# Where the last stage runs, in which order a sampled tile comes, and which router operand stands still

## What is computed

```python
# token mixer B: u, vb are two 512-wide projections of x
vn  = layer_norm(vb, ln_v_g, ln_v_b)
mix = einsum('gts,bcsgd->bctgd', tril(w_spatial), vn in chunks of 128) + b_spatial   # prompt
mix = w_spatial[:, 0, 0] * vn + b_spatial[:, 0]                                      # sampled
gm  = u * mix
merged = sigmoid(ga + gate_bias[0]) * (attn_out @ w_branch_a) + sigmoid(gb + gate_bias[1]) * (gm @ w_branch_b)
h = layer_norm(ALPHA * x + merged @ w_o, ln1_g, ln1_b)
# channel mixer: top-1 of 4 groups, top-2 of its 8 experts
lg = h @ w_router_group + b_router_group
le = h @ w_router_expert + b_router_expert
f  = sum over the two chosen experts of weight * (silu(h @ w_gate) * (h @ w_up)) @ w_down
y  = layer_norm(ALPHA * h + f, ln2_g, ln2_b)
```

## Time and profile before

| what | us |
|---|---|
| median of 3 runs (lowest, highest) | 1595.13 (1594.96, 1598.93) |
| the profiled execution | 1585.32 |
| its span, first to last instruction | 1583.8 |
| TensorE busy | 1440.6 |
| VectorE busy | 733.8 |
| TensorE's mean granted clock | 0.951 |

### The profile page before, as it was taken

One profiled execution on the slowest core, in us unless ns is written; L12 is line 12 of the kernel. 1 busy time (PEld: TensorE's weight loads), 2 busy tenths in 40 slices (PEclk: granted clock), 3 DMA queues, 4 the chain that ended last, 5 costly groups with the idle time before them and its releaser, 6 DMA issues. The chain is left out here.

```text
span 1583.8 us, 17679 instructions
## 1 busy us (share of the span) xinstructions
PE 1440.6 (91%) x5634; PEld 778.2 (49%) x5634; DVE 733.8 (46%) x1662; ACT 283.7 (18%) x620; POOL 254.5 (16%) x308
## 2 busy tenths in 40 slices
PE   7999999799979999998998898999299999999944
PEld 2444444344346666665776564555244444444410
DVE  0101023788888889932659445555311111111127
ACT  0100122112121111111564200000011111111112
POOL 3131000033310000101351000111111111111103
PEclk9999999799989999999999999999599999999967
DMA  9221001400021112201331394000189898989639
GB/s 313 63 64 33 15 15 67 126 0 1 0 96 69 60 60 86 76 28 38 98 109 57 114 355 195 27 27 27 45 339 351 339 349 337 354 334 348 249 92 249
DMA packets 74504, 221.88 MB, mean 140 GB/s; under 512 B 16738, under 2 KB 42338, under 8 KB 65098
## 3 DMA queue, kind: packets, MB, share of 16 engines
q1 hardware_dynamic: 58170, 184.64, 33.3%
q0 software_dynamic: 14992, 35.90, 6.4%
q10 hardware_dynamic: 1280, 0.53, 0.2%
HBM read 190.56 MB, written 38.84 MB: 145 GB/s over the span
## 5 line engine op out<-in xcount | busy, mean ns | idle before, releaser
L1713 PE MATMUL main_ps_experts<-w_gate_up,main_e_rowsT 128*128 128x512 f32 x512 | 227.7, 598 | 1.2 <-DVE main_e_rowsT L1812 1.2
L234 PE MATMUL ps_front<-front,x_all 128*128 128x512 f32 (+1 forms) x448 | 183.8, 566 | 1.7 <-ACT wi L364 1.7
L854 DVE TENSOR_SCALAR_CACHE_REDUCE front<-score,bound 128x384 bf16<-128x384 f32 (+2 forms) x198 | 174.2, 942 | 19.2 <-DVE bound L880 18.9
L1713 PEld LDWEIGHTS main_ps_experts<-w_gate_up,main_e_rowsT 128*128 128x128 f32 x512 | 95.7, 192 | 110.6 <-issue 110.6
L234 PEld LDWEIGHTS ps_front<-front,x_all 128*128 128x128 f32 x448 | 84.5, 193 | 93.8 <-issue 83.3
L1465 PE MATMUL ps_merge<-w_o,mergedT 128*128 128x512 f32 x256 | 118.4, 623 | 3.0 <-DVE h_rows L1586 3.0
L1817 DVE TENSOR_TENSOR main_hidden<-main_hidden,main_ps_experts 128x256 f32<-128x256 f32 x32 | 13.5, 421 | 221.1 <-ACT main_hidden L1766 221.1
L1740 PE MATMUL main_ps_experts<-w_down,main_hiddenT 128*128 128x512 f32 x256 | 115.3, 593 | 0.5 <-ACT main_hiddenT L1771 0.5
L712 PE MATMUL ps_gate<-x_all,w_gate 128*128 128x344 f32 x384 | 114.9, 458 | 0.3 <-ACT front L788 0.3
L712 PE MATMUL ps_gate<-x_all,front 128*128 128x344 f32 x384 | 113.2, 453 | 0.0
L712 PEld LDWEIGHTS ps_gate<-x_all,w_gate 128*128 128x128 f32 x384 | 73.5, 192 | 38.7 <-issue 1.2
(11 more groups left out here) (277 smaller groups left out, 1753.7 us busy)
## 6 DMA issues: line engine op xcount, KB each, us to landing
w_gate_up<-in_w_gate_up SPq DMA_DIRECT2D x32, 2048.0 KB, 9.1
w_down<-in_w_down SPq DMA_DIRECT2D x32, 1024.0 KB, 12.1
w_gate_up<-pair_out SPq DMA_DIRECT2D x16, 512.0 KB, 18.3
front<-in_w_qkvi SPq DMA_DIRECT2D x8, 930.0 KB, 12.7
w_gate<-in_w_gate SPq DMA_DIRECT2D x4, 1280.0 KB, 6.3
front<-in_w_gate SPq DMA_DIRECT2D x4, 1280.0 KB, 6.1
h_rows<-in_x_rows SPq DMA_DIRECT2D x9, 512.0 KB, 6.0
h<-h_rows SPq DMA_DIRECT2D x9, 512.0 KB, 2.6
```

What stands on the lines that cost most here:

```text
L234: mm = nc.tensor.matmul(ps[:, g % 2, 0:c1 - c0], x_all[:, k, t * P:(t + 1) * P], w[:, k, c0:c1], start=(k == 0), stop=(k == KC - 1))
L854: V.tensor_scalar(waste[0:n, at - width:at], s, column(bound, g), None, compare, ALU.add, accum_out=column(number, g)).then_inc(taken, 1)
L1713: mm = nc.tensor.matmul(ps[:, GU, :], rowsT[j][:, k, :], w_gu[jw][:, k, :], start=(k == 0), stop=(k == KC - 1))
```

## The change

Three edits.

1. **u/v stage.** The sampled tile comes first, as 32 matmuls of 256 columns, 8 rows high, of which four go to different partitions of one bank (`make_few`). ScalarE reads it into u and vb by itself, and has its moments without waiting for the constants. The loops become straight code. The mix of the last prompt tile and the transposes of the last two stand between the first matmuls of the gates (`last_mix`). The wait for `placed`, with the transposes behind it (`turn_places`), moves from ahead of the last two gate blocks to behind the second piece of six, and the row finding to behind the third to sixth, two each.

2. **Router.** `w_r` stands, hT moves: the logits come as 36 rows of 128. ScalarE copies them out (`lgT`), TensorE transposes them (`turn_logits`), VectorE adds the bias as before. The order per tile is project, route, rank, transpose of the logits.

3. **Last stage.** `finish` becomes a class, `Finish`, whose pieces are called at the end of each engine's list in the expert block. SyncE waits for all of `down` and for both scatter queues itself. TensorE puts ALPHA * h into the PSUM bank (`grow`: a 128x128 matrix ALPHA * identity, two tiles ahead) and adds the two results on top of it. ScalarE reads the finished sum with its row total, scales it to the mean and takes the squares. VectorE keeps the two products. The load of the longest list and its branch now come last; for lists over 128 rows the last stage runs once more (`finish_again`).

The diff, cut to its core:

```diff
 def choose_keys_and_gate
-            sp.wait_ge(normed, TILES)
-            sp.dma_start(outs["chunk_v"], vb[(TILES - 1) % 2][0:N_SAMPLE, :]).then_inc(chunk_out, 16)
-            sp.wait_ge(uv_full, TILES * 2)
+            sp.wait_ge(normed, 1)
+            sp.dma_start(outs["chunk_v"], vb[0][0:N_SAMPLE, :]).then_inc(chunk_out, 16)
+            sp.wait_ge(uv_full, 1 + NT * 2)
...
+            def make_few():
+                for k in range(KC):
+                    if k >= KC // 2:
+                        pe.wait_ge(w_uv_in[k], 16)
+                    for g in range(4):
+                        mm = nc.tensor.matmul(ps[g * FEW:g * FEW + N_SAMPLE, FEW_BANK, 0:QUARTER], x_all[:, k, SEQ:SEQ + N_SAMPLE],
+                                              w_uv(k)[:, g * QUARTER:(g + 1) * QUARTER], start=(k == 0), stop=(k == KC - 1))
+                mm.then_inc(uv_full, 1)
...
-            staggered(pe, TILES, [(0, make_uv), (1, mix), (2, turn)], loop=False)
-            pe.wait_ge(gm_read, TILES + 1)
+            make_few()
+            for i in range(1, TILES):
+                make_uv(i - 1)
+                if i >= 2:
+                    mix(i - 1)
+                    turn(i - 2)
+            def last_mix(at, which):
+                if (at, which) == (0, 2):
+                    turn(LAST - 1)
+                    mix(LAST)
+                if (at, which) == (1, 0):
+                    turn(LAST)
+                    pe.wait_ge(uv_read, 2 * NT)
+                if (at, which) == (2, 2):
+                    pe.wait_ge(gm_read, TILES)
...
-            pe.wait_ge(placed, 1)
-            for g in range(PAGES):
...
             def find_rows(at):
-                for b in ((0, 1), (2,), (3,), (4, 5), (6,), (7,))[at]:
+                if at == 1:
+                    turn_places()
+                for b in ((), (), (0, 1), (2, 3), (4, 5), (6, 7))[at]:
...
 def merge_and_route
-                    mm = nc.tensor.matmul(ps[:, 2, 0:ROUTER], hT[:, k, :], w_r[:, k, :], start=(k == 0), stop=(k == KC - 1))
+                    mm = nc.tensor.matmul(ps[0:ROUTER, 2, 0:P], w_r[:, k, :], hT[:, k, :], start=(k == 0), stop=(k == KC - 1))
                 mm.then_inc(routed, 1)
+            def turn_logits(i):
+                pe.wait_ge(lgT_read, i + 1)
+                nc.tensor.transpose(ps[:, 2, P:P + ROUTER], lgT, ident[0:ROUTER, 0:ROUTER]).then_inc(lg_turned, 1)
...
+                if 1 <= i <= TILES:
+                    route(i - 1)
                 if i >= 2:
                     rank(i - 2)
                 if 1 <= i <= TILES:
-                    route(i - 1)
+                    turn_logits(i - 1)
...
+                act.wait_ge(routed, t + 1)
+                if t >= 1:
+                    act.wait_ge(lg_turned, t)
+                nc.scalar.copy(lgT, ps[0:ROUTER, 2, 0:P]).then_inc(lgT_read, 1)
...
-                    dve.wait_ge(routed, i)
-                    V.tensor_tensor(logits[:, tiles[i - 1], :], ps[:, 2, 0:ROUTER], b_r[:], ALU.add).then_inc(logits_read, 1)
+                    dve.wait_ge(lg_turned, i)
+                    V.tensor_tensor(logits[:, tiles[i - 1], :], ps[:, 2, P:P + ROUTER], b_r[:], ALU.add).then_inc(logits_read, 1)
...
 def experts
+            if loaded:
+                sp.wait_ge(down, 2 * N_EXPERTS)
+                for j in range(2):
+                    sp.wait_ge(stored[j], 16 * N_EXPERTS // 2)
+                last.sync(sp)
...
 class Finish
+            def grow(t):
+                if t >= 4:
+                    pe.wait_ge(totalled, t - 3)
+                for c in range(2):
+                    nc.tensor.matmul(ps[:, 2 * (t % 4) + c, :], grown[:], h[:, t, c * 512:(c + 1) * 512], start=True, stop=False)
+            pe.wait_ge(grown_ready, 1)
+            grow(0)
             pe.wait_ge(spread_ready, 1)
+            grow(1)
             for t in range(NT):
                 pe.wait_ge(pairs_in[t], 32)
-                if t >= 4:
-                    pe.wait_ge(added, 1 + t - 3)
...
-                                              quads[t // 2][:, t % 2 * 2 + j, c * 512:(c + 1) * 512], start=True, stop=True)
+                                              quads[t // 2][:, t % 2 * 2 + j, c * 512:(c + 1) * 512], start=False, stop=True)
                 mm.then_inc(summed, 1)
+                if t + 2 < NT:
+                    grow(t + 2)
...
+                    act.wait_ge(summed, t + 1)
+                    nc.scalar.activation(hb, banks(t), ACT.Copy, accum_out=total[0:n, t:t + 1]).then_inc(totalled, 1)
+                    act.wait_ge(totalled, i)
+                    nc.scalar.mul(centre[0:n, t:t + 1], total[0:n, t:t + 1], -1.0 / D).then_inc(centred, 1)
...
-                V.scalar_tensor_tensor(hb, hb, ALPHA, more, ALU.mult, ALU.add,
-                                       accum_out=total[0:n, t:t + 1]).then_inc(added, 1)
...
 def build
-        experts(nc, ins, keep, scratch, 0, loaded=W_AHEAD, tag="main")
+        experts(nc, ins, outs, keep, scratch, 0, loaded=W_AHEAD, tag="main")
...
-                experts(nc, ins, keep, scratch, chunk, loaded=0, tag="rest")
-        finish(nc, ins, outs, keep, scratch)
+                experts(nc, ins, outs, keep, scratch, chunk, loaded=0, tag="rest")
+            finish_again(nc, outs, keep, scratch)
```

294 lines of the change are left out of this document (190 added, 104 removed).

## The result

| | before | after |
|---|---|---|
| median of the runs (range) | 1595.37 us (1594.96 to 1598.93) | 1573.26 us (1568.75 to 1573.50) |
| ratio, 95% interval | | 0.985, 0.9827 to 0.9872 |
| profiled execution, its span | 1585.32 us, 1583.8 us | 1573.19 us, 1571.7 us |

The change makes the kernel 22.1 us faster; the forecast was 36.6 and its range ended at 1571. Later groups of runs gave, kernel before against the change: 1585.9 to 1558.3 (ratio 0.9808, 0.9765 to 0.9851), 1599.2 to 1572.2 (0.9837, 0.9802 to 0.9871), 1585.6 to 1560.4 (0.9839) and 1599.0 to 1575.4 (0.985).

The account below looks back on a forecast made before the run. TensorE, busy 91% of the span, was taken as the bound, with transfers bounding the last stage. Terms -24.4 - 5.4 - 6.8 = -36.6 took the median from 1595.1 to 1558.5, rounded up to 1559 us; range 1551 to 1571.

Parts of the forecast that it names:

- Part 1: Sampled tile in the u/v stage: gates follow the prompt tiles at once, gaining 23.2 us until the last gate block.
- F: Time of the new small-tile matmuls (64 records, four side by side): 4.5 us taken; 4.0, 7.9 or 13.7 considered.
- Part 2: Last gate block: TensorE's meeting with VectorE's search moves behind two pieces; 24.4 us gained by the stage's end, 16.1 to 25.3.
- Nothing in the change makes VectorE faster: Last gate block: premise that VectorE's search still ends at 662.0 us, which caps the gain at 24.4 us.
- waits 0.8 us: Last gate block: TensorE arrives at 661.2 us and waits 0.8 us for VectorE's search.
- TensorE waits longer for VectorE: Sign in the last gate block that would show the forecast wrong; a wait under 2 us was expected.
- Part 3: Router in the merge stage: -4.0 at the stage's end, +2.0 for eight tiles, -3.4 for the clock; -5.4 us.
- long projection: Merge stage: projection slowed by the clock behind a routing, 15.68 us against 13.98; one taken instead of three, -3.4 us.
- the added stops: Router: ScalarE's read, a transpose and semaphores per tile, net +0.2 to +0.3 us each, +2.0 for eight.
- Part 4: Last stage: first transfer -7.4, end of program +1.3, work behind the last transfer -0.7; -6.8 us, between -3.5 and -8.9.
- +1.3, or +3.2: End of the program: the branch on the longest list costs 1.3 us there; 3.2 if GpSimd's drain costs its 5.3 too.
- The anchor: Whole kernel: sum made on the profiled span of 1583.8 us, its difference carried over to the median of 1595.1.

Follow-up runs that it names:

- a_vsp2: The whole change with attend's 16 GpSimd gathers of v rows replaced by plain SyncE loads from fixed places; 1561.19 us beside 1575.44 for the change.

## Why the prediction missed

- **Part 1** stood: TensorE's arrival in the last gate block was forecast at 661.2 and is 660.7. That is partly luck: F was 6.14 us, within 4.0 to 7.9 but 1.6 over the 4.5 taken, and from the small tile's end to the gates are 125.2 us, 2.2 less than the 126.4 of before and the 1.0 that was added for the small tile's transposes.
- **Part 2** failed at "Nothing in the change makes VectorE faster": it makes VectorE slower. It moves GpSimd's passes, and where they run decides how long VectorE's short steps take. The term "waits 0.8 us" measured 4.67, and 3.7 us of slow clock behind it had no term at all. These 7.5 us are the difference of 24.4 and 16.8, but for 0.1. The text named "TensorE waits longer for VectorE" as what would make it wrong, but gave no price to it, no chance, and no share of the range.
- **Part 3** was near, 5.3 to 6.8 us for 5.4, by misses that cancel. There is no long projection where one was taken (-1.7), the end of the stage gave 5.0 us and not 4.0, and the added stops cost 3.2 us and not 2.0. The weights were thought to give 1.4 net; they give between nothing and 1.6, and the order gives the rest.
- **Part 4** forecast -6.8 and measured -1.8 to -3.0 (last row of the table). The first transfer came 7.5 us sooner against the experts' end, as worked out, and the arithmetic behind the last transfer won 1.5 us in the first pair of profiles rather than 0.7 (0.1 to 1.5 against the other profiles of before). The failed term is "+1.3, or +3.2": the end takes 6.5 us longer, of which the drain has 1.5 and load and jump 4.9. The 1.3 was the price on SyncE's path, read at a place where the transfers hid TensorE's jump of 3.87 us; at the end of the program every engine's jump counts, and TensorE's is the last.
- **The anchor.** The profiled execution of before was 10 us quicker than the timed ones. That the two might be different levels was not asked. The sum didn't suffer, since both kernels have both levels, but the first comparison of the two profiles (12.1 us, of a short attend against a long one) would have led to a false cause.
- Of the rivals none came true. Stage by stage the change is worth 24 to 26 us; the forecast of -36.6 is 11 to 13 over that, by the two failed terms, 7.5 and 4 to 5, less the 0 to 1.4 that Part 3 gave beyond its share.

## What to carry to other kernels

When a wait for another engine is taken at its present length, ask what the change does to the neighbours of that engine: here a GpSimd pass over 512 columns stretched VectorE steps of 0.2 us to as much as 1.2, and a stop of TensorE of 4.7 us cost 8 with the slow clock behind it. Put the meeting behind work that can be had anyway (a third of a piece here, worth 7 us). When code moves to the end of the program, price it on every engine, the slowest of them above all: what one engine pays under another's transfers is free only there. And profile both kernels again before a difference is explained: one view of each showed a 13 us loss that the change had no part in.

## What the runs showed of the hardware

- GpSimd's drain at a block's end takes 0.082 to 0.085 us for each transfer that GpSimd issued in the block, gathers, scatters and plain loads alike, however long ago it landed: 5.37 us for 65, 5.28 for 64, 3.98 for 48, 2.67 for 32 (a_vsp2 leaves out 16 of the 48), 1.61 for 19. The first three rows are the change's first, attend and merge blocks, the fourth a_vsp2's attend block:

```profile
L70 POOLq DRAIN  x3: 40/140/5367, 133.1 to 295.3; - x3
...
L985 POOLq DRAIN  x3: 40/109/3977, 858.5 to 889.7; - x3
...
L1355 POOLq DRAIN  x3: 40/108/1613, 1126.4 to 1128.6; - x3
...
L985 POOLq DRAIN  x3: 40/114/2670, 847.0 to 876.8; - x3
```

  The change's last block has 64 as well; its 6.29 us begin while a GpSimd step of 0.94 still runs, and the 1.05 us in the last block of before, without a transfer, is that step. The drain is hidden if GpSimd has nothing to do at the end.
- A jump over the code that isn't run takes TensorE 3.3 to 4.5 us and the other engines 0.04 to 0.06, at either place. Ahead of the last stage it was hidden, and load and jump cost SyncE's path 1.3 us.
- ScalarE reads 1024 columns of PSUM with a sum in 1.02 us (and 0.19 for the sum); VectorE needed 1.21 for its pass over as many, which also scaled and added h.
- Sixteen router records move 128 columns against 36 stationary ones in 1.86 us, and moved 36 against 128 in 1.81; the difference was in the clock of what follows.
- In some groups of runs and not in others, VectorE's reads of PSUM started 2 to 4 us late and one of ScalarE's 1.9 us late beside GpSimd's gathers of v.
